# The decode samples' mixer moved from the end of an mLSTM/HGRN2 kernel into its first HGRN chunk

## The reference, cut to what matters

```python
def _layer(x, conv_buf, C, n, m, S, ...):
    mix, conv_buf, C, n, m, S = _mixer(x, conv_buf, C, n, m, S, ...)
    x = _layer_norm(DEEPNORM_ALPHA * x + mix, ln1_g, ln1_b)
    x = _layer_norm(DEEPNORM_ALPHA * x + _hmoe(x, ...), ln2_g, ln2_b)
# _mixer: z = x @ w_in + b_in; four mLSTM heads and four HGRN2 heads of 128 columns each
# one token of mLSTM:
num = (q.k) * w * v + dec * (q @ C);  qn = (q.k) * w + dec * (q . n)
h = num / maximum(abs(qn), exp(-m_t));  C_new = dec * C + w * outer(k, v)
# one token of HGRN2:
o = (q.k) * i + (q * exp(G)) @ S;       S_new = exp(G) * S + outer(k, i)
# both: rms norm by head, gate, out = concat @ w_out
# _hmoe: the best of 4 groups, in it the best 2 of 4 experts, silu(x@w1) * (x@w3) @ w2
```

## Time and profile before

| | us |
|---|---|
| median of 3 runs | 1246.21 (1244.73 to 1247.29) |
| the profiled execution | 1244.93 |
| its span, first to last instruction | 1243.0 |
| PE busy | 1057.4 (85%) |
| DVE busy | 587.7 (47%) |
| ACT, POOL busy | 278.2, 292.9 |
| mean granted clock of PE | 0.907 |

### The profile page before, as it was taken

One profiled execution on the slowest core, in us unless ns is written; L12 is line 12 of the kernel. 1 busy time (PEld: TensorE's weight loads), 2 busy tenths in 40 slices (PEclk: granted clock), 3 DMA queues, 4 the chain that ended last, 5 costly groups with the idle time before them and its releaser, 6 DMA issues.

```text
span 1243.0 us, 17536 instructions
## 1 busy us (share of the span) xinstructions
PE 1057.4 (85%) x6776; PEld 631.8 (51%) x6776; DVE 587.7 (47%) x964; ACT 278.2 (22%) x614; POOL 292.9 (24%) x262
## 2 busy tenths in 40 slices
PE   7999999799999679999999998844788899799400
PEld 4666666556565356566666655622344454355100
DVE  0550134447777675977787764387011111112046
ACT  2541121212112122232223221720111111111023
POOL 0000000001111332543454321154200001153175
PEclk9999999999999789999999997755699999899755
DMA  9010101100000700100000014003967798848396
GB/s 383 19 68 0 68 9 60 67 4 2 0 1 0 283 1 1 35 3 33 34 35 18 18 52 160 19 2 128 396 233 282 268 369 331 330 166 296 119 215 187
DMA packets 29288, 145.86 MB, mean 117 GB/s; under 512 B 5498, under 2 KB 5882, under 8 KB 20138
## 3 DMA queue, kind: packets, MB, share of 16 engines
q1 hardware_dynamic: 23546, 121.76, 25.9%
q0 software_dynamic: 5248, 18.94, 5.9%
q10 hardware_dynamic: 432, 4.34, 0.9%
HBM read 313.13 MB, written 23.79 MB: 271 GB/s over the span
## 4 chain that ended last, share of the span: by engine, by line
PE 76%; DMA 10%; DVE 8%; issue 2%; POOL 2%; SPq 1%; ACT 1%; DVEq 0%; ACTq 0%; POOLq 0%
PE psum L1612 17%; PE psum L616 9%; PE psum L599 9%; PE psum L1663 9%; PE psum L1296 5%; PE psum L1279 4%; PE psum L1301 4%; PE psum L635 4%; DMA weight_slots<-in_w_gate 3%; DMA x_cm<-y_slots,hg_k 2%; DMA scratch<-x_rows,hg_k 2%; PE psum L1630 1%; PE psum L1264 1%; PE psum L701 1%; POOL x_cm L1397 1%
## 5 line engine op out<-in xcount | busy, mean ns | idle before, releaser
L1612 PE MATMUL psum<-x_cm,weight_slots 128*128 128x344 f32 x720 | 209.0, 453 | 0.0
L1612 PEld LDWEIGHTS psum<-x_cm,weight_slots 128*128 128x128 f32 x720 | 136.6, 190 | 71.9 <-issue 1.1
L1663 PE MATMUL psum<-weight_slots,x_cm 128*128 128x512 f32 x256 | 113.7, 597 | 0.0
L1296 PE MATMUL psum<-weight_slots,scratch 128*32 128x256 f32 x1280 | 82.0, 413 | 19.8 <-DMA weight_slots<-in_w_gate 15.3
L1535 DVE SCALAR_TENSOR_TENSOR scratch<-scratch,psum 128x256 f32<-128x256 f32 x20 | 9.6, 480 | 157.9 <-PE psum L1301 157.9
L1279 PE MATMUL psum<-conv_qk,scratch 128*32 128x512 f32 x320 | 75.3, 614 | 10.2 <-DMA hg_q<-in_w_down 6.6
L1301 PE MATMUL psum<-conv_qk,scratch 128*32 128x256 f32 x640 | 74.2, 385 | 3.4 <-DMA hg_decay<-in_w_up 3.4
L891 POOL TENSOR_TENSOR scratch<-scratch,hg_k 128x256 f32<-128x256 f32 x56 | 46.0, 822 | 125.9 <-ACT scratch L787 125.8
L1663 PEld LDWEIGHTS psum<-weight_slots,x_cm 128*128 128x128 f32 x256 | 47.9, 192 | 54.3 <-issue 54.3
L1279 PE MATMUL psum<-hg_k,scratch 128*32 128x512 f32 x160 | 75.2, 614 | 0.0
L1279 PE MATMUL psum<-hg_q,scratch 128*32 128x512 f32 x160 | 75.2, 614 | 0.0
(11 more groups left out here) (369 smaller groups left out, 1802.9 us busy)
## 6 DMA issues: line engine op xcount, KB each, us to landing
weight_slots<-in_w_gate SPq DMA_DIRECT2D x80, 1024.0 KB
conv_qk<-in_w_up SPq DMA_DIRECT2D x40, 1024.0 KB
hg_decay<-in_w_up SPq DMA_DIRECT2D x40, 1024.0 KB
conv_qk<-in_w_down SPq DMA_DIRECT2D x40, 1024.0 KB
hg_k<-in_w_down SPq DMA_DIRECT2D x20, 1024.0 KB
hg_q<-in_w_down SPq DMA_DIRECT2D x20, 1024.0 KB
weight_slots<-in_w_in SPq DMA_DIRECT2D x6, 2048.0 KB, 8.0
y_slots<-scratch SPq DMA_DIRECT2D x20, 512.0 KB, 7.6
```

The costliest lines, as they stand in the source:

```text
L1296: m = mm(PS[lane, 2, 0:FF], xgT[i][:, k, lane], w_gate[q][:, k], start=(k == 0), stop=(k == KD - 1))
L1612: i = mm(PS[0:m, idx % 4, 0:PIECE], lhs_of(k), xT[:, k, n * PIECE:(n + 1) * PIECE], start=(k == 0), stop=(k == KD - 1))
L1663: i = mm(PS[:, bank, :], xT[:, k, c * P:(c + 1) * P], w_slot(g)[:, k, :], start=(k == 0), stop=(k == KD - 1))
```

## The change

**The samples' mixer** moves forward. Their second product of w_in stands on PE after the mLSTM chunks, and bias is now added to rows, not to columns. Their gates and q, k products stand on DVE inside the last mLSTM chunk; the dots, heads and norm in HGRN chunk 0; their mix and output projection in chunk 1. The dots are column-tiled: head h writes to partitions 32h to 32h + 31, so four heads' dots may run side by side, and the result is turned by one transpose. SP loads both states for this into the two weight slots that w_out takes later, so w_out is loaded after the dots; ln_gb, the norm's gains, is too, as q_apart lies in its place.

**The row order** is now samples, tile 0, 1, ..., 7: chunk 1 handles the samples' row, chunk c from 2 on tile c - 2 as before. Tile 7 has a row buffer of its own and is loaded in the last chunk. Tiles 6 and 7 get their norm's gain and shift on DVE (residual_norm_alone), not on POOL.

**The states' updates** move into the expert steps 0 to 15, as three DVE operations each. The states are loaded a second time, by ACT after the last chunk's projection. The samples' v rows go to DRAM in chunk 0 and come back in eight pieces of 8 rows, each broadcast to all partitions (load_v), one for two updates. The outer products, their copies and POOL's updates are gone. S_s is stored before pair 8. SP's and DVE's steps are no longer loops.

The core of the diff:

```diff
+        sp.wait_ge(s.zs_proj, 1)
+        sp.wait_ge(s.zs_row, 4)
         sp.dma_start(bias, t["b_row"][:, 1024:2048].partition_broadcast(P).rearrange("p a n -> p (a n)")).then_inc(s.bias2_in, 16)
+        for kind, name in enumerate(("C0", "S0")):
+            sp.dma_start(states_early[kind], t[name].rearrange("p h b v -> p (h b) v")).then_inc(s.state_in, 16)
+        store_v_rows(0)
         sp.dma_start(w_r, t["w_r"]).then_inc(s.mixer_in, 16)
...
+        sp.wait_ge(s.zs_row, 8)
+        store_v_rows(1)
+        sp.wait_ge(s.num_rows, 2)
         sp.dma_start(w_out, t["w_out"].rearrange("(e p) n -> p e n", p=P)).then_inc(s.mixer_in, 16)
...
+    def samples_sums(pe, kind):
+        pe.wait_ge(s.dots_in, kind + 1)
+        if kind == 0:
+            nc.tensor.matmul(PS[:, 4, 0:2 * HB], ones, SC[:, 5632:5632 + 2 * HB], start=True, stop=True)
+        else:
+            nc.tensor.matmul(sums[2], ones, TH[0], start=True, stop=True)
+    def samples_dots(pe, kind):
+        pe.wait_ge(s.dots_in, kind + 1)
+        pe.wait_ge(s.state_in, 32)
+        for b in range(NS):
+            for h in range(H):
+                e = h * NS + b
+                i = nc.tensor.matmul(PS[32 * h:32 * h + 32, DOTS_BANK[kind], 256:256 + P], q_apart[kind][:, e * 32:(e + 1) * 32],
+                                     states_early[kind][:, e], start=(b == 0), stop=(b == NS - 1))
+        i.then_inc(s.num_rows, 1)
...
+    def samples_gates(dve, link, tell):
+        v, hb = nc.vector, by_hb
+        a, dd, dec, nm = T[7], T[8], T[9], T[10]
+        li, lf, mb = gs[:, :, 0], gs[:, :, 1], gs[:, :, 2]
...
+        link(v.tensor_tensor(hb(dec), mb, hb(T[6]), ALU.subtract))
+        link(v.tensor_tensor(hb(T[21]), hb(T[6]), lf, ALU.add))
+        tell(v.tensor_scalar(nm, T[21], -1.0, None, ALU.mult), s.sgates_arg)
+        dve.wait_ge(s.masks_made, 1)
+        for q in q_apart:
+            link(v.memset(q, 0.0))
+        dve.wait_ge(s.qk_silu, 9)
+        qs, ks = conv_ps[:, 0:HB], conv_ps[:, HB:2 * HB]
+        link(v.tensor_copy(spread_q(0), hb(qs)))
+        link(v.tensor_tensor(T[0], qs, ks, ALU.mult))
+        tell(v.tensor_tensor(T[1], qs, n0, ALU.mult), s.dots_in)
+    def samples_keys(dve, link, tell):
+        v, hb = nc.vector, by_hb
+        dd, dec = T[8], T[9]
+        ks = conv_ps[:, HB:2 * HB]
+        kS, qS = K[:, :, NP_:NT], Q[:, :, NP_:NT]
+        link(v.tensor_tensor(hb(TH[0]), qS, kS, ALU.mult))
+        dve.wait_ge(s.sgates_exp, 2)
+        link(v.tensor_tensor(hb(TH[2]), qS, hb(TH[14]), ALU.mult))
+        tell(v.tensor_copy(spread_q(1), hb(TH[2])), s.dots_in)
+        link(v.tensor_scalar(dd, dd, KSCALE, None, ALU.mult))
...
+    def samples_heads(dve, link, tell, kind):
+        v, hb = nc.vector, by_hb
+        dd, dec, nm = T[8], T[9], T[10]
...
+            link(v.scalar_tensor_tensor(T[17], T[16], -1.0, nm, ALU.mult, ALU.max))
+            link(v.tensor_tensor(T[16], T[16], T[17], ALU.max))
+            link(v.reciprocal(T[16], T[16]))
+            link(v.tensor_tensor(hb(T[17]), turned_dots(0), hb(dec), ALU.mult))
+            link(v.tensor_tensor(T[15], T[15], T[4], ALU.mult))
...
+        def project_out_samples():
+            pe.wait_ge(s.mixS_ready, 2)
+            pe.wait_ge(s.mixer_in, 16 * 4)
+            for e in range(8):
+                for j in range(4):
+                    i = mm(PS[32 * j:32 * j + NS, 6, 0:256], mixS[:, e, :], w_out[:, e, j * 256:(j + 1) * 256], start=(e == 0), stop=(e == 7))
+            i.then_inc(s.mixed, 1)
...
+                    if l == 0:
+                        samples_sums(pe, 0)
+                        samples_sums(pe, 1)
+                    if l == 3:
+                        samples_turn(pe, 2, zrow[1], 5)
+                        samples_dots(pe, 0)
+                    if l == 4:
+                        samples_dots(pe, 1)
+                    if l in (5, 6):
+                        turn_dots(pe, l - 5)
+                    if l == 7:
+                        samples_squares(pe)
+                if c == 1 and l == 1:
+                    project_out_samples()
...
-        samples_product(pe, 0, (7, 6))
+        turn_outputs(NCH - 1)
+        for part in range(4):
+            project_out(NCH - 1, part)
...
-        act.wait_ge(s.zs_proj, 2)
-        act.dma_start(C0, t["C0"].rearrange("p h b v -> p (h b) v")).then_inc(s.state_in, 16)
-        act.dma_start(S0, t["S0"].rearrange("p h b v -> p (h b) v")).then_inc(s.state_in, 16)
+        act.wait_ge(s.i_proj, NCH)
+        act.dma_start(C0, t["C0"].rearrange("p h b v -> p (h b) v")).then_inc(s.state_back, 16)
+        act.dma_start(S0, t["S0"].rearrange("p h b v -> p (h b) v")).then_inc(s.state_back, 16)
...
-        def add_outer(m):
-            part = (C0, S0)[m // 8][:, 4 * (m % 8):4 * (m % 8) + 4, :]
-            pool.wait_ge(s.outer_read, m + 1)
-            tell(g.tensor_tensor(part, part, kv_outer[m % 3].rearrange("p (a v) -> p a v", a=4), ALU.add), s.state_added)
...
+        def residual_norm_alone(c):
+            row = xrow_of(c)
+            link(v.scalar_tensor_tensor(row, row, mv[:, 0:1], ln_gb[:, 0], ALU.subtract, ALU.mult))
+            dve.wait_ge(s.lstd_ready, place(c) + 1)
+            dve.wait_ge(s.x1_ready, place(c))
+            v.scalar_tensor_tensor(row, row, lstd, ln_gb[:, 1], ALU.mult, ALU.add).then_inc(s.x1_ready, 1)
...
+                        dve.wait_ge(s.bias2_in, 16)
+                        samples_rows(dve, link, 2, 6, zrow[1])
+                    if l == 4:
+                        samples_gate(dve, link, 0)
+                    if l == 5:
+                        samples_columns(dve, tell, 2, 5)
+                    if l == 7:
+                        samples_heads(dve, link, tell, 0)
+                    if l == 8:
+                        samples_heads(dve, link, tell, 1)
+                        samples_gate(dve, link, 1)
+                if c == 1 and l == 2:
+                    samples_mix(dve, link, tell, 0)
+                    samples_mix(dve, link, tell, 1)
...
-        samples_rows(dve, link, 2, 0, zrow[1])
+        residual_sum(NCH - 2)
+        outputs_gate(NCH - 1)
         state_update(NCH - 1)
-        residual_sum(NCH - 2)
-        for q in q_apart:
-            link(v.memset(q, 0.0))
-        outputs_gate(NCH - 1)
+        residual_norm_alone(NCH - 2)
         logits(NCH - 3)
-        residual_norm(NCH - 2)
...
+        residual_norm_alone(NCH - 1)
         logits(NCH - 2)
...
+        def load_v(piece):
+            if piece >= 1:
+                sp.wait_ge(s.state_added, 2 * piece)
+            sp.dma_start(v_piece, v_dram[piece:piece + 1].rearrange("a (b v) -> a b v", b=NS).partition_broadcast(P).rearrange("p a b v -> p (a b) v")).then_inc(s.v_piece_in, 16)
...
-        for q, expert, _ in first[:2]:
-            load_down(q, expert, None)
+        load_v(0)
...
+                    load_v(pair)
                 sp.wait_ge(s.up_done, pair * 2 + (i + 1))
...
+        def update_state(n):
+            kind, piece, at = n // 8, n // 2, 4 * n % HB
+            part, rows = (C0, S0)[kind][:, at:at + 4], v_piece[:, 4 * (n % 2):4 * (n % 2) + 4]
+            spread = lambda ap: ap[:, at:at + 4].unsqueeze(2).to_broadcast([P, 4, P])
+            dve.wait_ge(s.v_piece_in, 16 * (piece + 1))
+            dve.wait_ge(s.state_back, 32)
+            link(v.tensor_tensor(part, part, spread(decay_state[kind]), ALU.mult))
+            link(v.tensor_tensor(rows, rows, spread(k_state[kind]), ALU.mult))
+            tell(v.tensor_tensor(part, part, rows, ALU.add), s.state_added)
...
+        samples_product(pe, 6, (7, 6))
         samples_turn(pe, 1, zrow[0], 1)
...
+                samples_gates(dve, link, tell)
             dve.wait_ge(s.h_sq, c + 1)
```

522 lines of the change are left out of this document (222 added, 300 removed).

## The result

| | before | after |
|---|---|---|
| median (lowest to highest), us | 1246.75 (1244.73 to 1248.17) | 1207.8 (1207.29 to 1210.07) |
| profiled execution, us | 1244.93 | 1207.56 |
| its span | 1243.0 | 1205.4 |
| ratio of the times, 95% interval | | 0.970 (0.969 to 0.972) |

The forecast was 1202 us with a range of 1190 to 1221. The span was forecast at 1199.0 and is 1205.4, a miss of 6.4 us. The marks of the two traces show where it lies. Each is the start of the same work in both; the third column is the difference, the last what the prediction's terms make of it at that mark.

The account below looks back on a forecast made before the run. PE was taken to bound the chunks, VectorE chunk 0's second half, PE or weights the expert steps. Additions 16.8, mixer end -44.3, routing -17.5 and experts +1 made -44.0 us: 1202 us, range 1190 to 1221.

Parts of the forecast that it names:

- The start: Between the mLSTM chunks and level 0 of HGRN chunk 0: the samples' gates, keys and second product add 3.6 us.
- Chunk 0: HGRN chunk 0: turn and dots add 2.7 us in the PE-bound first half, heads and gate 5.3 in the VectorE-bound second.
- the heads' price of 5.3: Second half of chunk 0: 18 small VectorE operations take 4.3 us, plus 1.0 for meeting GpSimd's level scaling.
- One sign of being wrong: In chunk 0: VectorE's heads taking above 5 us would show the forecast wrong.
- Chunks 1 and 2: HGRN chunks 1 and 2: samples' output projection, turn and wait for the mix add 4.5 us, routing the samples 0.7.
- The end of the mixer: From the last chunk to the last tile's logits: these end at about 775.4 in place of 819.65, 44.3 us gained.
- Routing: Routing before the experts: without GpSimd's updates beside them, VectorE's 44 small operations run at 0.20 us, saving 17.5 us.
- The rival that had routing slow for another reason: Routing before the experts: the change doesn't give the 17.5 us saving, so 1220 us; chance 6%.
- The expert steps: Expert stage: updates hidden at 0, v loads +5.8, store of S_s -5.8 at pair 5 and +1 at pair 8; net +1 us.
- The expert stage pays for every byte: Expert stage: v costs 11.6 us and the moved 2 MB 5.8 at their new place, so 1218 us; chance 10%.
- Contention in chunk 0: Chunk 0 and head of chunk 1: all 36 added small VectorE operations take 0.6 us beside GpSimd, +14, 1216 us; chance 15%.
- The slow case: Expert steps: loads of v landing 20 us after issue hold VectorE and cost 64 us, so 1266 us; chance 4%.

Follow-up runs that it names:

- the two experiments: Kernel before with GpSimd's updates of the samples' states left out, 1226.5 us; kernel after with 30 GpSimd operations added beside VectorE's routing, 1229.2 us.

## Why the prediction was right, and where it was off

**The start: +3.6 forecast, +5.5 seen** at the first project_in (427.05 in place of 421.54). Of this, 1.1 us are there at the first samples_product, before anything that was changed, and are scatter between executions: in the fourteen traces that product starts between 403.7 and 405.8. The remaining 4.4 are the term plus 0.8. The 0.8 is in the head transposes, which come 3.95 us later behind that product and not 3.1: of the nine small operations ahead of them, one met GpSimd's squares and took 0.97 us in place of 0.19.

```profile
412.22 0.97 DVE L638 TENSOR_TENSOR scratch<-scratch,small 128x32 f32<-128x32 f32 x1
```

```profile
412.10 1.04 POOL L1871 TENSOR_TENSOR scratch<-scratch 128x512 f32<-128x512 f32 x1 [12.91 <-DVE scratch L1994]
```

The second product took 4.5 us in place of the 3.64 that I charged, at the low clock behind the idle stretch, and level 0 behind it 1.06 in place of 1.92. The trace of after drew one of the quick ones: in the seven traces where the product took 5.9 to 6.1 us, the start costs 5.2 to 5.5 and not 4.4.

**Chunk 0: +8.0 forecast, +6.2 seen** from there to o_num. The dots took 1.96 of the 2.2, and the heads' price of 5.3 is confirmed by moving them (5.6). Part of the difference is the clock again: before, the first three products of project_in took 2.77 us at the low level (the earlier trace rows has level 0 at 1.92), and now the second samples_product takes that stretch. I had said that it isn't counted twice, and over both terms it wasn't; I only put it in the wrong one. That the sum is near is partly luck, for the pieces measured singly don't add up to it: 0.5 for the turn, twice 1.96 for the dots, 5.6 for the heads, less some 1.3 for the clock, make 8.7 where 6.2 are seen, and the 2.5 between aren't accounted for. One sign of being wrong did show, if barely: the heads' 18 operations fill 5.2 us of VectorE's time (3.5 from 452.9 on and 1.7 from 462.8 on), above the 5 that I had set. The sentence that the second dots lie in time that PE waits anyway is refuted by the exchanged loops, where the second group cost as much as the first.

**Chunks 1 and 2: +5.2 forecast, +6.6 seen.** The wait for the mix is 1.28 and not 0.4; the other 0.5 isn't accounted for.

**The end of the mixer: -44.3 forecast.** From o_num of the last chunk to the first reduction, 83.3 us before are 39.4 after: -43.9. The row buffer's part in it was right in kind, tile 6 no longer holding up tile 7, and measured at 4.6.

**Routing: -17.5 forecast, -17.8 seen.** This was the term that the diff doesn't name, and the two experiments show its mechanism from both sides. The rival that had routing slow for another reason is excluded.

**The expert steps: +1 forecast; here a step failed.** The net was made of +5.8 for v, -5.8 for taking the store of S_s from pair 5, and +1 at its new place. Six traces with the whole new stage have 267.4 us on average from hid 0 to hid 19 (265.6 to 269.4), two of the old stage 262.5: 4.9 more. Of these the loads of v are about 3.5, 2.6 by the medians for seven pieces and about 1 in the first step (14.6 us on average in the six traces, 13.5 in the two). The third is 1.9, the price in the step from 16 to 17. The first was on the high side (5.8 for 3.5), which hid part of the miss. What failed is the second, "-5.8 there", since "DMA is full". I had read the full stretch of the earlier trace rows and charged each byte in it. But the store is issued at 1031.6, and what matters is whether it delays the weights of a step in which PE waits for them, and that is the step from 12 to 13, whose gate loads are issued at 1058.2. Here is the trace of before just ahead of that, and under it the first half us of the last row:

```profile
1049.00:1052.00 3.00, 3.00 (x32) 1.38 (x34) 0.69 (x1) 0.60 (x1) 1.17 (x2) 1.00 1.05 418
1052.00:1055.00 3.00, 3.00 (x42) 1.28 (x38) 1.02 (x2) 0.60 (x1) 0.00 (x0) 1.00 0.91 377
1055.00:1058.00 3.00, 3.00 (x64) 1.82 (x56) 0.00 (x0) 0.39 (x1) 0.00 (x0) 1.00 0.86 253
...
1055.00:1055.50 0.50, 0.50 (x18) 0.27 (x10) 0.00 (x0) 0.00 (x0) 0.00 (x0) 1.00 0.42 172
```

PE is busy for all of it, and from 1055.0 the engines' share falls to 0.42 and their rate to 172 GB/s from 418: they have nearly caught up, so the 2 MB were absorbed before the awaited loads were issued. The steps from 11 to 13 take 34.2 us on average in the two kernels with the store there (33.4 and 35.0) and 33.3 in the two that have neither the store nor the later pieces of v (33.1 and 33.6). So the store cost about 0.9 us and not 5.8. Of the 0.9, 0.4 is in the step from 11 to 12 (12.53 and 12.63 against 12.14 twice); the rest isn't parted from the scatter, but 5.8 is far outside it. With 3.5 + 1.9 - 0.9 = 4.5 the term would have been within half a microsecond of the mean of the traces, and the forecast at 1205 to 1206 us. The profiled execution itself drew a slow one of these stages, 268.8, which is another 1.4; at its end it got 1.6 back, from the last hid on (86.4 us, the low end of the 86.4 to 89.3 of all traces).

**The rivals.** "The expert stage pays for every byte" priced v at 11.6 us and the store at 5.8; both are refuted. Contention in chunk 0 was given +14: VectorE's small operations there and at the head of chunk 1 show it singly (0.39, 0.60 and 0.61 in place of 0.19), one ahead of the head transposes costs the 0.8 above, and the heads cost 0.3 more than forecast. The slow case, v landing late, needed 17.5 us from issue to landing; the median is 8.6, with one piece at 24.7, the first, which VectorE awaited 0.9 us; its longest wait for v is 8.0.

## What to carry to other kernels

Before moving work off a busy path, look at what the same work does to the engines that only run beside it: here a background update on GpSimd cost VectorE 18 us in a chain that had no data in common with it, nearly half the gain. Look at each kind of instruction, for a scaling on GpSimd cost the same engine next to nothing. Price a transfer not by how full the DMA engines are where it is issued but by whether the queue is still backed up when the next weights are asked for that an engine waits for: the same 2 MB cost about 0.9 us well ahead of such weights and 1.9 just ahead of them. And when work is moved into idle time, put it where the other engine is the bound: the same 18 small operations cost 5.6 us in chunk 0 and about 1 in chunk 1.

## What the runs showed of the hardware

- A VectorE operation of 128x36 elements with two SBUF inputs took up to 1.30 us beside back-to-back GpSimd tensor_tensor operations of 1.26 us, and 0.20 without them; reductions, a reciprocal and a copy out of PSUM were not slowed (0.19, 0.21, 0.31).
- VectorE operations of 128x512 with two SBUF inputs took 0.68 to 0.99 us inside a GpSimd tensor_scalar of 128x1024 (2.8 us each), and 0.69 without it.
- 64 products of 128x32 by 128 columns took 1.96 us with neighbours on different column groups and 5.96 with neighbours on the same (and the same rows of PSUM): 31 against 93 ns each.
- With gate loads that ended 8.97 us after their issue the next 64 products took 5.32 us, with 7.25 us they took 3.66.
- Steps that wait for DMA scatter by 1.5 to 2.5 us from one execution to the next (the step from 0 to 1: 13.7 to 16.2 where the code is the same), so that one profile prices nothing in them that is smaller.
- The second samples_product, 64 instructions, took 4.5 us in four traces and 5.9 to 6.1 in seven, with the same order of work around it.
